# A two-layer backbone step on one core: chunk 2's scan products before half of the z rows, conditioning pieces between z rows, and z's gate by Exp and Ln

## What is computed

```python
def layer_step(x, mod, ...):
    sh1, sc1, g1, sh2, sc2, g2 = split(mod, 6)          # mod = silu(c) @ w_ada + b_ada
    h = rmsnorm(x, n1) * (1 + sc1) + sh1
    a_q, a_k, a_v, b_q, b_k, b_v, z, xbc, dt_raw = split(h @ w_in)
    o_a, o_b = attention of group A (windowed, with a sink) and of group B (q and k normalised)
    o_c = rmsnorm(y * silu(z), ssm_g)                   # y: bidirectional chunked scan of xbc, dt
    x = x + g1 * (concat(o_a, o_b, o_c) @ w_out)
    h = rmsnorm(x, n2) * (1 + sc2) + sh2
    return x + g2 * hier_moe(h)                         # top-1 of 4 groups, top-2 of 4 experts
# the scan, for each chunk, head and direction
y_diag = (C B^T * decays) @ (x dt)                      # inside the chunk
state  = B^T @ (decays to the end * x dt)               # what the chunk leaves to the next
y_off  = C @ (entering state) * decays from the start   # needs the states of other chunks
```

## Time and profile before

| | us |
|---|---|
| median of 3 runs (lowest, highest) | 775.5 (774.59, 776.07) |
| the profiled execution | 778.39 |
| its span | 776.5 |
| PE busy in the span | 742.7 (96%) |
| DVE busy | 581.0 (75%) |
| ACT busy | 506.7 (65%) |
| POOL busy | 50.4 (6%) |
| mean granted TensorE clock | 0.991 of full speed |

### The profile page before, as it was taken

One profiled execution on the slowest core, in us unless ns is written; L12 is line 12 of the kernel. 1 busy time (PEld: TensorE's weight loads), 2 busy tenths in 40 slices (PEclk: granted clock), 3 DMA queues, 4 the chain that ended last, 5 costly groups with the idle time before them and its releaser, 6 DMA issues.

```text
span 776.5 us, 10986 instructions
## 1 busy us (share of the span) xinstructions
PE 742.7 (96%) x4022; PEld 574.6 (74%) x4022; DVE 581.0 (75%) x964; ACT 506.7 (65%) x842; POOL 50.4 (6%) x36
## 2 busy tenths in 40 slices
PE   5999999899999999999999999988999999999994
PEld 2557877458976788888879788845798788888883
DVE  4158477887656889999868746878766789999965
ACT  3038784475456877778756678557556887777854
POOL 0001342000000000000000135200000000000000
PEclk8999999999999999999999999999999999999998
DMA  9963033978328899999855112196731199999912
GB/s 356 423 260 109 1 135 102 424 290 322 112 109 328 319 379 367 348 375 376 316 235 213 57 53 92 45 375 222 296 139 55 54 331 381 373 357 367 360 52 85
DMA packets 34062, 186.22 MB, mean 240 GB/s; under 512 B 5200, under 2 KB 6608, under 8 KB 17104
## 3 DMA queue, kind: packets, MB, share of 16 engines
q1 hardware_dynamic: 34000, 185.42, 63.2%
HBM read 182.79 MB, written 2.62 MB: 239 GB/s over the span
## 4 chain that ended last, share of the span: by engine, by line
PE 76%; DVE 11%; ACT 7%; issue 4%; DMA 0%; DVEq 0%; ACTq 0%; SPq 0%
PE psum L903 23%; PE psum L1065 11%; PE psum L932 11%; PE psum L1267 5%; PE psum L1030 5%; PE psum L722 3%; PE psum L964 3%; PE psum L881 2%; DVE att L2335 1%; PE psum L785 1%; PE psum L1237 1%; PE psum L1135 1%; ACT split L1471 1%; PE psum L916 1%; PE psum L1149 1%
## 5 line engine op out<-in xcount | busy, mean ns | idle before, releaser
L2124 DVE TENSOR_TENSOR split<-ring,split 128x2048 fp32r<-128x2048 f32 x96 | 219.8, 2290 | 26.7 <-ACT split L1602 25.3
L1602 ACT CAST split<-ring 128x2048 fp32r<-128x2048 f32 x96 | 183.6, 1913 | 22.3 <-PE psum L932 14.4
L903 PE MATMUL psum<-split,y_hi 128*128 128x512 f32 x512 | 160.8, 395 | 0.4 <-ACT selT L1575 0.4
L903 PEld LDWEIGHTS psum<-split,y_hi 128*128 128x128 f32 x512 | 93.7, 188 | 18.6 <-issue 0.4
L903 PE MATMUL psum<-split,y_lo 128*128 128x512 f32 x256 | 100.1, 391 | 0.0
L1065 PE MATMUL psum<-ring_r,hT_hi 128*128 128x512 f32 x216 | 73.2, 393 | 0.0
L932 PE MATMUL psum<-split,hidT 128*128 128x512 f32 x256 | 69.4, 393 | 0.0
L932 PEld LDWEIGHTS psum<-split,hidT 128*128 128x128 f32 x256 | 47.3, 188 | 12.1 <-DVE hidT_lo L2129 2.5
L903 PEld LDWEIGHTS psum<-split,y_lo 128*128 128x128 f32 x256 | 48.1, 188 | 10.2
L2566 POOL TENSOR_TENSOR ud<-const,da_hi 128x1024 fp32r<-128x1024 f32 x12 | 27.3, 2292 | 395.6 <-DVE da_lo L2225 388.1
L1065 PEld LDWEIGHTS psum<-ring_r,hT_hi 128*128 128x128 f32 x216 | 40.0, 188 | 9.0 <-issue 0.8
(11 more groups left out here) (324 smaller groups left out, 1433.0 us busy)
## 6 DMA issues: line engine op xcount, KB each, us to landing
ring<-in_w_gu SPq DMA_DIRECT2D x64, 1024.0 KB, 6.8
ring<-in_w_ada SPq DMA_DIRECT2D x40, 1024.0 KB, 6.7
ring<-in_w_down SPq DMA_DIRECT2D x32, 1024.0 KB, 6.9
ring<-in_w_rows SPq DMA_DIRECT2D x12, 1024.0 KB, 5.0
ring<-in_w_out SPq DMA_DIRECT2D x8, 1024.0 KB, 5.0
ring<-in_first SPq DMA_DIRECT2D x7, 1024.0 KB, 13.8
ring<-in_w_xbc SPq DMA_DIRECT2D x8, 800.0 KB, 8.7
par<-in_par SPq DMA_DIRECT2D x1, 1728.0 KB, 12.4
```

Of the source, the lines that this page charges most:

```text
L903: last = pe.matmul(dst, x[:, g, t, :], w[:, j, :], start=(t == 0 and i == 0), stop=(t == KD - 1 and i == 2))
L1602: act.copy(splits[unit_split(n)][:, 0, :], slot(key)).then_inc(raised("whi", l, p), 1)
L2124: tt(lo, slot(unit_key(l, p, n)), hi.bitcast(F32), ALU.subtract).then_inc(raised("wlo", l, p), 1)
```

## The change

Four edits, in both layers:

1. `ssm_y 2`, `ssm_off 1` and `ssm_off 2` come before two thirds of the second half of the z rows: `ssm_y 2`, `rows 5 0`, `ssm_off 1`, `ssm_off 2`, `rows 5 1`, `rows 5 2`, then the scores. Before, `ssm_y 2` came after the rows, and the two `ssm_off` between the scores of pairs 1 to 3.
2. Three `ada` pieces stand between z rows (after `rows 4 1`, `rows 4 2` and `rows 5 0`). The three (layer 0) or two (layer 1) pieces in a row ahead of the scores go, and the others are spread evenly over the attention, not with more at its start. With `AHEAD_OF_SCORES = 3` and `("scores", PAIRS // 2)` the slots 0 to 2 of the ring stay in use for pieces until the middle of the attention; `last_use` of four slots is set so that the planner gives them out as they come free.
3. z's gate is z * exp(-ln(1 + exp(-z))), tile by tile, in two steps: `gate_in m` (ACT: Exp into `z_exp`; POOL: min with 1e30 and + 1) and `gate_sigmoid m` (ACT: Ln, then Exp; POOL: `z * z_exp`). `z_exp` lies where `xs` and `xdd` were. The table loads go.
4. The banks of the moved products are chosen by hand (`beyond_rows`), counted from the bank of the last z rows.

```diff
@@ layer_steps
-    s += [("ssm_y", 1), ("ssm_in", 2), ("w_split", 5), ("rows", 4, 0), ("seg", 2), ("rows", 4, 1), ("rows", 4, 2), ("turn_qk", 1), ("prep", 2)]
-    s += [("rows", 5, m) for m in range(TILES)] + [("ssm_y", 2), ("silu_z",)]
-    burst = 6 if l else 3
-    s += ada[early:burst]
+    s += [("ssm_y", 1), ("ssm_in", 2), ("w_split", 5), ("rows", 4, 0), ("seg", 2), ("rows", 4, 1), ada[early], ("rows", 4, 2), ada[early + 1],
+          ("turn_qk", 1), ("prep", 2)]
+    s += [("ssm_y", 2), ("rows", 5, 0), ("gate_in", 0), ada[early + 2], ("ssm_off", 1), ("ssm_off", 2), ("gate_sigmoid", 0)]
+    s += [("rows", 5, 1), ("gate_in", 1), ("rows", 5, 2)]
+    spent = early + AHEAD_OF_SCORES
     heads = head_steps()
+    at = heads.index(("scores", 1))
+    heads[at:at] = [("gate_sigmoid", 1), ("gate_in", 2)]
     at = heads.index(("scores", 2))
-    heads[at:at] = [("ssm_off", 1)]
-    at = heads.index(("scores", 3))
-    heads[at:at] = [("ssm_off", 2)]
+    heads[at:at] = [("gate_sigmoid", 2)]
...
-    rest = ada[burst:8] + [("ada_turn", l, 1)] + ada[8:14]
+    rest = ada[spent:8] + [("ada_turn", l, 1)] + ada[8:14]
...
-        want = min(len(rest), len(rest) * (i + 1) * 3 // (len(heads) * 2)) if i < len(heads) // 3 else \
-            len(rest) // 2 + (len(rest) - len(rest) // 2) * (i + 1 - len(heads) // 3) // (len(heads) - len(heads) // 3)
+        want = len(rest) * (i + 1) // len(heads)
@@ build
-            if s == ("scores", 0):
+            if s == ("scores", PAIRS // 2):
                 first_late = len(pieces)
...
+        if key[0] == "w_hi" and key[2] == 5:
+            for i, k in enumerate((("h_hi", key[1], 0), ("h_hi", key[1], 1), key, ("win", key[1], 5))):
+                last_use[place[k]] = n + AHEAD_OF_SCORES + 0.1 * (i + 1)
...
+        def beyond_rows(l, n):
+            return (uses["row", l, 0, 2][0] + n) % 7
@@ PE: ssm_off
-                            pe.wait_ge(*fill(("yoff", l, m, g)))
+                            pe.wait_ge(*fill(("yoff", l, m, g), beyond_rows(l, (5, 6, 1, 2)[2 * m - 2 + g])))
...
+                        turn[0] = beyond_rows(l, 4)
@@ ACT
-                    elif kind == "silu_z":
-                        for m in range(TILES):
-                            act.wait_ge(*taken(("row", l, m, 2)))
-                        act.activation(z, z, ACT.Silu).then_inc(sig["zs"], 1)
-                        act.preload_act_table_set("natural_log_exp_and_others")
+                    elif kind == "gate_in":
+                        m = arg[0]
+                        act.wait_ge(*taken(("row", l, m, 2)))
+                        act.wait_ge(*full(("ydiag", l, 2)))
+                        act.wait_ge(*full(("state", l, 2)))
+                        act.activation(z_exp[:, m, :], z[:, m, :], ACT.Exp, scale=-1.0).then_inc(sig["z_act"], 1)
+                    elif kind == "gate_sigmoid":
+                        m = arg[0]
+                        act.wait_ge(sig["z_pool"], per["z_pool"] * l + 2 * m + 1)
+                        act.activation(z_exp[:, m, :], z_exp[:, m, :], ACT.Ln).then_inc(act_step, 1)
+                        act.wait_ge(act_step, act_steps())
+                        act.activation(z_exp[:, m, :], z_exp[:, m, :], ACT.Exp, scale=-1.0).then_inc(sig["z_act"], 1)
@@ POOL
+                    if step[0] == "gate_in":
+                        m = step[1]
+                        pool.wait_ge(sig["z_act"], per["z_act"] * l + 2 * m + 1)
+                        pool.tensor_scalar(z_exp[:, m, :], z_exp[:, m, :], 1e30, 1.0, ALU.min, ALU.add).then_inc(sig["z_pool"], 1)
+                    elif step[0] == "gate_sigmoid":
+                        m = step[1]
+                        pool.wait_ge(sig["z_act"], per["z_act"] * l + 2 * m + 2)
+                        tt(z[:, m, :], z[:, m, :], z_exp[:, m, :], ALU.mult).then_inc(sig["z_pool"], 1)
```

13 lines of the change are left out of this document (8 added, 5 removed).

## The result

The changed kernel takes 788.57 us (median of 4; 786.59 to 789.99) beside 775.05 for the kernel before (774.41 to 776.07): a ratio of **1.0148, 95% interval 1.0131 to 1.0166**, which is 11.5 us. The two medians themselves lie 13.5 us apart; against the medians of the kernel before beside the experiments (776.14 to 776.97) it is 11.6 to 12.4, so I use the 11.5 of the ratio. The forecast was 777.2, in a range that ended at 780.0. The direction is right and the size is not. The profiled execution took 789.99, the slowest of the four, with a span of 787.6, 11.1 more than the one before.

A forecast was written before the change was run, and what follows sets the result against it. PE bounds the kernel, so only its waits count: 9.25 us against 8.4 is +0.85, with +0.8 for the pieces +1.65, added to the 775.5 median: 777.2 us, range 772.5 to 780.0.

The forecast's parts named there:

- What bounds the kernel: PE, busy 96% of the span; the change can win only PE's waits, 8.4 us in the two attention stretches.
- Edit 1, no term: Moved scan products cost PE nothing: `ssm_off` at 131.9 without a wait, 0.7 us to spare; the `turn 2` wait goes.
- Edit 2, +0.8 us: Pieces standing alone 0.5, changes back to rows 0.4, less 0.1 for `ssm_off`; no transfer wait, `ada_turn` wait gone.
- Edit 3, the wait at `scores 3`: ACT's copies of `turn_qk 2` queue behind the gate's chain, with POOL's step at 0.6 us; PE waits 2.45 us per layer.
- the other waits: Besides 2.45 at `scores 3`: 0.25, 0.2 and 0.65 in layer 0; 1.2, 0.6, 0.75 and 0.7 in layer 1.
- 1.65 forecast: Net loss over both layers: +0.85 us of PE waits (9.25 against 8.4) and +0.8 us for the pieces.
- Faster: Rival, chance 0.22: copies of `turn_qk 2` start by 5.6 us after the first scores, waits 5.05 in all, 772.9 us.
- The lock between POOL and DVE: Rival, chance 0.10: POOL's and DVE's operations block each other in the first pairs, +2.4 us on the forecast, 779.6 us.
- its sign: Test of the lock between POOL and DVE: it decides if POOL's products are above 1.3 us in the attention.
- The pieces were not late: Rival, chance 0.04: the third piece lands 10 us after its release, PE stands 3 us before `ssm_off` per layer, 783 us.
- What would show it: Tests: 2 to 3 us wait at pair 3's scores, copies at 6 to 7 us, `scale` waits under 1 us a layer.

The follow-up runs named there:

- e7: e5 with the conditioning pieces back in a burst ahead of the scores of pair 0, the old spread and the old ring slots: 786.84 us, ratio 1.0123.
- e5: The changed kernel without POOL's min and + 1 (Ln takes 1 as bias) and with `gate_sigmoid 2` behind pair 2's exponentials: 778.09 us, ratio 1.0019.
- e13: e5 with, in layer 1, one conditioning piece moved from the rows to behind the scores of pair 1, and seven filling matmuls: 776.52 us, ratio 0.9988.
- e1: The changed kernel with 18 matmuls whose result nobody reads put ahead of the scores of pair 3 in both layers: 783.42 us, ratio 1.0088.
- e2: The changed kernel with `gate_sigmoid 2` moved behind the exponentials of pair 2, so the copies of `turn_qk 2` come first: 778.06 us, ratio 1.0016.
- e4: The changed kernel without its gate edit: one Silu with two table loads, no POOL work on z: 782.84 us, ratio 1.0079.

## Why the prediction was wrong

**What bounds the kernel** was read rightly: no matmul was added, and all that came of it was waits and PE's pace. One reading was off: the waits for `scale` are 4.6 of 8.4 us, over half and not nearly half.

**Edit 1, no term, `ssm_off` at 131.9 with 0.7 us to spare.** It stood at 131.76 and waited for nothing, and the `turn 2` wait went. Right, but the spare time was 0.4 and not 0.7 (DVE's timeline, then PE's):

```profile
130.95 0.42 DVE L2328 TENSOR_TENSOR hin<-psum,hin 128x256 f32<-128x256 f32 x1
...
131.76 0.71 PE L1188 MATMUL psum<-par,xbc 64*128 64x256 f32 x4
```

DVE's last operation for `ssm_off` ended at 131.37. Without the three pieces ahead of it, `ssm_off` waits 1.9 us (e7).

**Edit 2, +0.8 us.** No wait on a transfer, and `ada_turn`'s wait gone: right. The size was too small. In layer 0 of e5, where both kernels ran at full clock, the waits are 1.8 us instead of 3.6, but the two stretches together (58.93 + 41.64) are only 0.46 shorter than before (55.79 + 45.24). So the reordered rows and pieces cost 1.3 us there and not 0.4. PE's timelines, added up from start to start, show where. Up to `scores 0` the rows take 33.83 us for 33.12, the pieces 2.98 for 2.71 and the transposes of `turn_qk` 1.37 for 1.24; `ssm_off` took 2.04 in its new place, for 2.15. The 1.0 for a piece alone was right, and a change back to rows costs 0.10 to 0.13. What the forecast had at nothing is the way out of the rows: the last row matmul ahead of a piece takes 0.32 us instead of 0.23, three times; with two more changes back this explains 0.5 of the rows' 0.7. The rest of the 1.3, some 0.3, lies behind `scores 0`. Layer 1 I can only estimate, from e13, which ran at full clock there: its two stretches are 0.2 longer than before, with 2.6 less of waits and 1.5 of filling matmuls, which leaves 1.3 as well.

**Edit 3, the wait at `scores 3`.** The mechanism was right in each link: ACT's queue, POOL before Ln, the copies behind it, the bank. The failed step is "with one input in the place of two I halve the slope: 0.6 us". It measured 2.03, outside both bounds (0.29 and 1.39). I had bounded an operation that no row showed by rows of another instruction, and took for granted that fewer inputs means less time. Put 2.0 and the product's 1.3 into the forecast's own sum, and the copies start 8.2 us after the first scores, which is what the trace shows (147.68 less 139.47); the wait becomes 4.15, for a measured 3.97. This term is 1.55 us a layer; the other waits came out 0.85 shorter in all than forecast (11.5 is the sum, for 9.25), so waits explain 2.25.

**The missing step: the clock.** This is the larger failure: no term and no rival had it, and the sum took PE's pace as fixed. The kernel before had a granted clock of 1.00 in its attention in spite of 8.4 us of waits, and I took that as given. The new wait is one piece of 4 us in the place of several of 0.3 to 1.4. The matmuls behind it ran at the lower level, and with the wait filled they gave 2.1 and 1.4 us back (e1), with another 1.6 behind the router in the profiled execution.

Together: 1.65 forecast, + 2.25 of waits, + 3.4 for the clock, + 1.8 for rows and pieces, + 1.6 behind the router, are 10.7 against 11.1 in the span and 11.5 in the ratio. The sum is an estimate: the 1.8 takes layer 0's 1.3 for both layers, and the 1.6 is the weakest item, since it comes and goes between kernels that have the same work there. How near it comes is partly luck.

**The rivals.** "Faster" rested on the copies starting by 5.6 us after the scores. With the queue mended they start at 4.8 (e2), and the kernel is still not faster, since the rows and pieces took what the waits gave. The lock between POOL and DVE was set to decide at POOL products above 1.3 us in the attention. There they took 1.26 to 1.27 in both layers; the mean of 1.32 comes from tile 0's, 1.43, beside DVE's sums for `ssm_off`. So its sign wasn't met. Its mechanism is there, in the 1.11 us of L2362, but nothing waited for that, and filling the wait (e1) or moving one step of ACT (e2), neither of which touches the lock, gave back 4.7 and 10.2 of the 11.5 us. e5 doesn't test it: its POOL products remain, and the same operation takes 1.2 there. The pieces were not late.

**What would show it.** Three of the tests came out: a wait at the scores of pair 3 put down to ACT, no wait before `ssm_off`, none on a transfer. Four did not: that wait was 4.0 and not 2 to 3, the copies came at 8.2 us and not at 6 to 7, the waits for `scale` in layer 1 were 1.7 and not under 1, and the rows were slower than 0.1 for each change. No test on the list looked at the clock.

## What to carry to other kernels

When a chain of small steps over two engines goes into the queue of an engine that also serves PE, put what PE waits for ahead of each link that waits for the other engine. Here one step moved was worth 10 us, and the price of the slow link didn't matter any more. Price a wait on PE twice, for itself and for the pace of the matmuls behind it, as a risk and not as a rule (layer 0 of e4 had no second price), and when an edit takes work away from a stretch, ask what its waits were hidden by: edits that lose 1% without each other can be neutral together.
